# A two-block transformer forward pass on one core: the state-space stage's decay factors, with the subtraction moved into the exponential's bias and the exponentials one pair ahead

## The reference, cut to what matters

```python
A_cs = jnp.cumsum(A, axis=-1)
seg = A_cs[..., :, None] - A_cs[..., None, :]
Lmat = jnp.exp(jnp.where(tril, seg, -jnp.inf))
CB = jnp.einsum('bclgn,bcsgn->bcgls', Cc, Bc)
y_diag = jnp.einsum('bcgls,bgecls,bcsgep->bclgep', CB, Lmat, X)
```

## Time and profile before

| what | value |
|---|---|
| runs | 1759.41, 1753.83, 1754.40 us; median 1754.4 |
| span of the profiled execution | 1752.2 us |
| PE busy | 1714.4 us, 98% |
| PE weight loads busy | 1600.3 us, 91% |
| DVE busy | 1359.9 us, 78% |
| ACT busy | 999.9 us, 57% |
| POOL busy | 680.6 us, 39% |
| memory read | 285.18 MB, 163 GB/s over the span |

### The profile page before, as it was taken

One profiled execution on the slowest core, in us unless ns is written; L12 is line 12 of the kernel. 1 busy time (PEld: TensorE's weight loads), 2 busy tenths in 40 slices (PEclk: granted clock), 3 DMA queues, 4 the chain that ended last, 5 costly groups with the idle time before them and its releaser, 6 DMA issues.

```text
span 1752.2 us, 30797 instructions
## 1 busy us (share of the span) xinstructions
PE 1714.4 (98%) x12360; PEld 1600.3 (91%) x12360; DVE 1359.9 (78%) x2072; ACT 999.9 (57%) x1558; POOL 680.6 (39%) x417
## 2 busy tenths in 40 slices
PE   9989999988999999999999999999999999999997
PEld 8989999987999989999778999999999877899997
DVE  6858877566687869985797699787996599669795
ACT  6475545684654554576564566456477556366462
POOL 7631104961310166344474511038344366431113
PEclk9999999999999999999999999999999999999999
DMA  8435555541455554464345455555455235545552
GB/s 293 146 113 180 193 175 176 193 128 54 145 188 185 179 180 160 158 211 142 104 145 189 148 181 189 179 185 176 150 181 182 97 130 182 181 144 193 184 178 85
DMA packets 80926, 288.23 MB, mean 164 GB/s; under 512 B 9104, under 2 KB 9360, under 8 KB 80656
## 3 DMA queue, kind: packets, MB, share of 16 engines
q1 hardware_dynamic: 79776, 283.15, 49.0%
q10 hardware_dynamic: 1008, 3.11, 0.5%
HBM read 285.18 MB, written 1.05 MB: 163 GB/s over the span
## 4 chain that ended last, share of the span: by engine, by line
PE 92%; DVE 4%; ACT 2%; issue 1%; DMA 0%; POOL 0%; SPq 0%; DVEq 0%; ACTq 0%; POOLq 0%
PE lin L718 24%; PE lin L720 23%; PE lin L719 23%; PE lin L745 4%; PE logit L745 4%; PE logit L746 2%; PE lin L746 2%; PE stat L834 1%; PE stat L1237 1%; PE tr L1237 1%; ACT w_hi L1302 1%; PE logit L1200 1%; PE logit L1109 1%; PE logit L1131 1%; PE logit L1033 1%
## 5 line engine op out<-in xcount | busy, mean ns | idle before, releaser
L1302 ACT ACTIVATE w_hi<-w_raw 128x1024 fp32r<-128x1024 f32 (+1 forms) x546 | 537.8, 1033 | 352.0 <-PE lin L720 249.6
L514 POOL TENSOR_TENSOR w_lo<-w_raw,w_hi 128x1024 fp32r<-128x1024 f32 (+1 forms) x197 | 473.5, 2415 | 337.6 <-ACT w_hi L1302 234.2
L514 DVE TENSOR_TENSOR w_lo<-w_raw,w_hi 128x1024 fp32r<-128x1024 f32 (+1 forms) x349 | 482.5, 1387 | 33.2 <-ACT w_hi L1302 31.0
L718 PE MATMUL lin<-h_pair,w_hi 128*128 128x256 f32 x1424 | 407.4, 286 | 3.3 <-DVE h_pair L523 2.4
L718 PE MATMUL lin<-hid_pair,w_hi 128*128 128x256 f32 x1408 | 402.1, 286 | 2.2 <-DVE hid_pair L523 1.7
L719 PE MATMUL lin<-h_pair,w_hi 128*128 128x256 f32 x1424 | 402.8, 283 | 0.0
L720 PE MATMUL lin<-h_pair,w_lo 128*128 128x256 f32 x1424 | 402.8, 283 | 0.0
L719 PE MATMUL lin<-hid_pair,w_hi 128*128 128x256 f32 x1408 | 398.3, 283 | 0.0
L720 PE MATMUL lin<-hid_pair,w_lo 128*128 128x256 f32 x1408 | 398.3, 283 | 0.0
L718 PEld LDWEIGHTS lin<-h_pair,w_hi 128*128 128x128 f32 x1424 | 273.0, 192 | 6.0 <-issue 3.9
L719 PEld LDWEIGHTS lin<-h_pair,w_hi 128*128 128x128 f32 x1424 | 273.1, 192 | 1.1 <-issue 0.7
(11 more groups left out here) (368 smaller groups left out, 3038.1 us busy)
## 6 DMA issues: line engine op xcount, KB each, us to landing
w_raw<-in_upA SPq DMA_DIRECT2D x112, 512.0 KB, 3.9
w_raw<-in_upB SPq DMA_DIRECT2D x64, 512.0 KB, 4.2
w_raw<-in_xbc SPq DMA_DIRECT2D x48, 512.0 KB, 4.4
w_raw<-in_dnA SPq DMA_DIRECT2D x32, 512.0 KB, 3.6
w_raw<-in_dnB SPq DMA_DIRECT2D x32, 512.0 KB, 3.7
w_raw<-in_z SPq DMA_DIRECT2D x32, 512.0 KB, 4.4
w_raw<-in_gates SPq DMA_DIRECT2D x32, 512.0 KB, 4.1
w_raw<-in_ps SPq DMA_DIRECT2D x32, 512.0 KB, 3.9
```

The source lines that it names most:

```text
L514: eng.tensor_tensor(w_lo[slab.slot][:, half, part], w_raw[slab.slot][:, half, part], w_hi[slab.slot][:, half, part].bitcast(F32), ALU.subt ...
L718: nc.tensor.matmul(out, lhs[0], rhs[0], start=first, stop=False)
L1302: nc.scalar.activation(w_hi[slab.slot][:, half, part], w_raw[slab.slot][:, half, part], ACT.Copy)\
```

## The change

It touches four engines' lists and adds one small tile.

- VectorE: `ssd_seg` becomes two operations for a pair of heads, each of 2x128 columns. They take the minimum of the spread sum and the row's own sum. The one for the second half of rows writes `decay`, the one for the first half writes back into `logit`, over its first 128 columns; the other 128 columns of `logit` need no minimum and are left.
- ScalarE: each head's exponential becomes two operations, one of 256 columns from `logit` and one of 128 columns in `decay`, each with the negated sum as its bias (`neg_cum`, written once for a layer by one operation of 128x64).
- `running_sums(c + 2)` now waits for the exponentials of pair c (`ssd_exp`), before it waited for `ssd_seg(c)`.
- Order on ScalarE: pairs 0 and 1 first; then for each m pair 2m+2, the rounding, pair 2m+3 (at m = 0 the rounding comes before pair 2).
- Order on VectorE: sums two pairs ahead (`ssd_seg(c + 2)`), and last in the round; the split of half 1 directly behind `ssd_m(c)`, ahead of `ssd_out(c - 1)`.
- Order on GpSimd: the split of half 0 between the two gates.

```diff
@@ gates_weights (GpSimd)
                     if n >= 1:
                         ssd_gate(2 * n - 1, 1)
+                    split_lo(pool, slab.ahead(SPLIT_AHEAD), 0)
                     ssd_gate(2 * n, 0)
-                    split_lo(pool, slab.ahead(SPLIT_AHEAD), 0)
@@ running_sums (TensorE)
                     if c >= 2:
-                        pe.wait_ge(s.ssd_seg, SH * l + 2 * c - 2)
+                        pe.wait_ge(s.ssd_exp, SH * l + 2 * c - 2)
@@ xbc_conv (ScalarE)
                         act.wait_ge(s.dt_tr, l + 1)
+                        nc.scalar.activation(neg_cum_sb[:, :], tr[:, 2 * SH:4 * SH], ACT.Copy, scale=-1.0)
                         nc.scalar.activation(dt_tok_sb[:, :], tr[:, 0:4 * SH], ACT.Copy).then_inc(s.dt_tok, 1)
@@ state-space stage (ScalarE)
+                act.wait_ge(s.dt_tok, l + 1)
+
+                def ssd_decay(c):
+
+                    act.wait_ge(s.ssd_seg, XCH * l + c + 1)
+                    for head in (2 * c, 2 * c + 1):
+                        nc.scalar.activation(decay[:, head % 4, 0:T], logit[:, head % 4, :], ACT.Exp, bias=neg_cum[:, 0, head:head + 1])
+                        nc.scalar.activation(decay[:, head % 4, T:T + P], decay[:, head % 4, T:T + P], ACT.Exp,
+                                             bias=neg_cum[:, 1, head:head + 1]).then_inc(s.ssd_exp, 1)
+
+                ssd_decay(0)
+                ssd_decay(1)
                 for m in range(XCH // 2):
-                    for head in range(4 * m, 4 * m + 4):
-                        act.wait_ge(s.ssd_seg, SH * l + head + 1)
-                        nc.scalar.activation(decay[:, head % 4, :], decay[:, head % 4, :], ACT.Exp).then_inc(s.ssd_exp, 1)
+                    if 1 <= m < XCH // 2 - 1:
+                        ssd_decay(2 * m + 2)
                     done(slab_at("gates", m, l))
+                    if m == 0:
+                        ssd_decay(2)
+                    if m < XCH // 2 - 1:
+                        ssd_decay(2 * m + 3)
@@ ssd_seg (VectorE)
-                    for head in (2 * c, 2 * c + 1):
-                        for t, (lo, n) in enumerate(((0, T), (T, P))):
-                            ins = ts(decay[:, head % 4, lo:lo + n], logit[:, head % 4, T - n:T],
-                                     dt_tok[:, 1, t, head:head + 1], 0.0, ALU.subtract, ALU.min)
-                        ins.then_inc(s.ssd_seg, 1)
+                    at = 2 * (c % 2)
+                    for t, out in ((1, decay[:, at:at + 2, T:T + P]), (0, logit[:, at:at + 2, 0:P])):
+                        cum_here = dt_tok[:, 1, t, 2 * c:2 * c + 2].unsqueeze(2).to_broadcast([P, 2, P])
+                        ins = tt(out, logit[:, at:at + 2, t * P:t * P + P], cum_here, ALU.min)
+                    ins.then_inc(s.ssd_seg, 1)
@@ ssd_group and its calls (VectorE)
-                        if c + 1 < XCH:
-                            ssd_seg(c + 1)
                         ssd_m(c, j)
+                        if j % 2:
+                            weights(slab_at("gates", c // 2, l))
                         if j >= 1 or not first:
                             ssd_out(c - 1, j + 3)
-                        if j % 2:
-                            weights(slab_at("gates", c // 2, l))
+                        if c + 2 < XCH:
+                            ssd_seg(c + 2)
                 ssd_seg(0)
+                ssd_seg(1)
```

More of the change, by code:

```diff
@@ L395, in build @@
         dt_tok = dt_tok_sb[:, :].rearrange("p (i t h) -> p i t h", i=2, t=2)
+        neg_cum_sb = sb("neg_cum_sb", [P, 2 * SH])
+        neg_cum = neg_cum_sb[:, :].rearrange("p (t h) -> p t h", t=2)
         small = sb("small", [P, 64])
```

## The result

| | before | changed |
|---|---|---|
| median of 5 runs, us | 1754.14 (1753.81 to 1759.41) | 1759.22 (1758.75 to 1763.41) |
| ratio, 95% interval | | 1.0031 (1.0018 to 1.0044) |
| span of the profiled execution, us | 1752.2 | 1761.6 |

The changed kernel is 0.3% slower. Both kernels have some runs 4 to 6 us above their others, which is why medians are compared. The profiled execution was the longest of its five, 4.2 us above their median: between 400 and 450 us TensorE's granted clock was 0.90 where it was 1.00 before, and the stage's first running sums come at 845.09 and not 840.90. That is 4.19 later, and 4.17 of it is there at the first instruction that the change adds (the new copy, at 736.12; the copy that stood in its place before started at 731.95).

A forecast was written before the change was run, and what follows sets the result against it. TensorE, busy 98% of the span, was taken to bound the kernel, with at most some 2.2 us to win. The opening's 0.2 loss, all else 0, added to 1754.4 gave 1754.6 us; range 1751.5 to 1758.0.

The forecast's parts named there:

- TensorE needs four things from the others in each round of a slab and two pairs: Steady rounds, some 8.0 us: exponentials before sums, product before y, splits before slab, `ssd_out` before `CB`; all cost 0.
- 6.2 of 8.0: ScalarE's load in a steady round: rounding 1.91, four heads 2.76, `gate_sig` some 0.5, at times a square some 1.0.
- Spare 4 us: Steady rounds: pair 3's and 4's exponentials end well before TensorE wants them, hiding 17 us more ScalarE work.
- The opening: Start of the stage: y(1)'s wait shrinks 0.63, a new 0.72 wait follows; loss 0.09 a layer, 0.2 in all.
- The estimate by the errata's table: Opening's exponentials from the skill's cycle table: 0.65 a head, so a loss of 0.02 a layer; the rows' 0.69 decided.
- The steady rounds' other terms: Exponentials, product before y (VectorE freed 20 us, hidden), splits, and output before `CB`: each taken as 0.
- The splits' order: Steady rounds: splits are made two slabs ahead, GpSimd's may move a few us either way; cost 0.
- Rival 1: VectorE's split, held by GpSimd's, delays the output before `CB`: 0.5 at six places, +3 us, 1757.6; chance 0.13.
- rival 2: Exponentials late everywhere, if over 1.2 us a head uses up the 4 us spare: 1760 and more; chance 0.02.
- TensorE still busy all of the long stretch: Sign to check in the changed kernel: no idle TensorE from the second slab to the last y.

The follow-up runs named there:

- Experiment 1: Changed kernel with the tanh `gate_sig(m - 2)` moved back directly behind the rounding, ahead of pair 2m+3's exponentials: 1753.79 us, ratio to before 0.9991.
- experiment 8: Changed kernel with the tanh ahead of pair 2m+3's exponentials, and pair 2's exponentials ahead of the rounding behind slab 0: 1753.35 us, ratio to before 0.9998.
- experiment 3: Changed kernel with both splits back: VectorE's behind `ssd_out`, GpSimd's behind both gates; all else kept: 1768.46 us, ratio to before 1.0081.
- experiment 5: Changed kernel with VectorE's split alone back behind `ssd_out`: 1768.57 us, ratio to before 1.0084.
- experiment 6: Kernel before with the arithmetic alone changed (two minima, two biased exponentials, sums waiting for exponentials), no queue rearranged: 1772.27 us, ratio to before 1.0098.

## Why the prediction was wrong

The forecast was 1754.6, the range 1751.5 to 1758.0; the time is 1759.22. Its cause is one step.

- **The step that failed** is the sentence "TensorE needs four things from the others in each round of a slab and two pairs". It needs a fifth: two free banks before each even slab. The list was made of data (exponentials, product, split, `CB`'s output) and left out space. `gate_sig` appeared in it only as load, "a `gate_sig` of some 0.5", in a sum of ScalarE's time in a round, 6.2 of 8.0. Experiment 1 shows that the load is harmless and the place isn't. The trace of the kernel before held the answer: tanh until 876.18, slab at 876.61, with 1.3 us to be put ahead of that tanh.
- **The sum of ScalarE's time hid it.** "Spare 4 us" was right for the exponentials: the running sums waited in no round but the first. A spare of an engine in a round says nothing about the spare of one instruction in its queue, and this one had 0.33.
- **The opening** was right in kind and nearly in size. y(1) was to be idle about 0.5: 0.48. The sums of pair 4 were to wait 0.72: 0.58. The net loss was to be 0.09 a layer: 0.01. The terms behind it: two minima 0.68 until the product, measured 0.67 (852.21 to 852.88); a head's exponentials 0.69 from start to start, measured 0.65 to 0.67 (879.93, 880.60, and the tanh behind them at 881.25). The estimate by the errata's table, 0.65, that the prediction drew from the Trainium skill (VectorE: DVE Perf Modes, section on the TRN2 errata) is nearer to that and to the net loss than the 0.69 from this kernel's rows. It changed nothing in the result.
- **The steady rounds' other terms** were 0 and came out as 0: no wait before a y behind y(1), none for a split, none before `CB` (0.18 in experiment 8 only). ScalarE is up 15.4 in all, forecast 17. VectorE, 53.06 busy in the stretch, is at 49.99, and down 10.4 in all, where the prediction freed 20: the minima (26.8 us in all, before 44.3) and the products (33.0, before 48.0) give back 32.5, and VectorE's splits, now held by GpSimd's, take 22.7 more in the whole execution (505.2, before 482.5). Experiment 1, which has all of this, shows no loss from it.
- **The splits' order** was costed at nothing because "they are made two slabs ahead". For the slab that reads them that holds. What VectorE's split leans on wasn't asked: experiments 3 and 5 show that its new place is worth 9 us to the changed order, because the minima, the exponentials and the tanh stand behind it.
- **Rival 1** named VectorE's queue and the wait before `CB`. It was the wrong wait. No rival had ScalarE's queue ahead of a slab, and the chance of 0.06 for a loss over 0.3% was 2% rival 2 and a third of rival 1, neither of which took place.
- **The range** had two loose ends. It took 0.7 for the scatter between runs whose two times, 1753.83 and 1754.40, are 0.57 apart, and its upper end lies 0.4 over the 1757.6 of rival 1 without a reason. With either put right 1759.22 is still outside.
- The prediction's own test, "TensorE still busy all of the long stretch", found it at once: 56.82 of 58.80.

## What to carry to other kernels

When instructions move in an engine's queue, ask for every instruction that stands behind them what it releases: results, and also the buffer or bank that it was the last to read. Spare is a property of that one instruction, from its end to the moment when its waiter is due, and the busy share of its engine over a round doesn't show it. A wait that the profile gives as "issue" at an instruction that begins to fill a ring's buffer is a place to look for a late reader; here four were, while the waits for a tanh at the end of the stage had their releaser named.

## What the runs showed of the hardware

- **TensorE's clock behind short waits.** In experiment 3 the granted clock fell to half (0.50 from 879 to 881 us), that is to 1.2 GHz, some 1.2 us after the end of a wait of 2.12, while the engine was running again. It stayed there some 3.3 us and cost 1.64. Behind the waits before 897.78 and 1451.42 it fell in the same way, 1.2 and 0.5 us after their end. Of the four waits of that length one, at 1432.51, had no fall behind it (clock 1.00 from 1425 to 1442). In experiment 5 it is the same: a fall behind three of the four, and none behind the one at 1433.97. Why that one is spared the traces don't show. Waits of 0.99 had none (clock 1.00 in 855.70 to 914.50 of the changed kernel), and waits of 1.85 to 1.95 in experiment 6 neither (the clock was 1.00 from 862 to 915). So the price of an idle microsecond isn't fixed: 9.2 us for 4.5 us more of waiting.
- **Contention followed the order.** In the changed kernel VectorE's split starts while GpSimd's is running, and takes 3.42 instead of 1.21; it ends 1.09 after GpSimd's. The product that was held for 2.55 before takes 1.04 (857.97), and the minima 0.42 each. GpSimd's split takes 3.11 instead of 2.40, and this isn't from meeting VectorE's: in experiment 5 the two don't meet (VectorE's takes 1.22), and GpSimd's, at 853.72, still takes 3.11. What both cases have is a product of VectorE that started 0.19 before it, where in the kernel before the product started 0.66 after it. Changed kernel, VectorE, then GpSimd:

```profile
858.94 3.42 DVE L516 TENSOR_TENSOR w_lo<-w_raw,w_hi 128x1024 fp32r<-128x1024 f32 x1
...
858.16 3.11 POOL L516 TENSOR_TENSOR w_lo<-w_raw,w_hi 128x1024 fp32r<-128x1024 f32 x1
```
